# A decoder step on one core: the 128-fold copy of the relative-bias rows is made in DRAM from a 12 KB scratch

## The reference, cut to what matters

```python
def run_layer(x, c, mixer, w_ada, b_ada, ...):
    sh1, sc1, gt1, sh2, sc2, gt2, sh3, sc3, gt3 = adaln_params(c, w_ada, b_ada)   # silu(c) @ w_ada + b_ada
    x = x + MACARON * gt1 * swiglu(modulate(x, g_ffn1, sh1, sc1), w1_ffn1, w3_ffn1, w2_ffn1)
    heads, state = mixer(modulate(x, g_mix, sh2, sc2))
    x = x + gt2 * (heads @ w_out)
    x = x + MACARON * gt3 * swiglu(modulate(x, g_ffn2, sh3, sc3), w1_ffn2, w3_ffn2, w2_ffn2)
```

```python
    b = bias[jnp.clip(delta, 0, nk)]          # delta = query - key, bias = rel_bias[bucket of the distance]
    s = s + jnp.transpose(b, (2, 0, 1))
```

## Time and profile before

| | us |
|---|---|
| median of 3 runs | 2632.72 (2629.66 to 2635.13) |
| the profiled execution, its own time | 2627.94 |
| its span, first to last instruction | 2625.9 |
| around the span | 2.0 |
| TensorE busy | 2461.6 (94% of the span) |
| VectorE / ScalarE / GpSimd busy | 1163.8 / 905.3 / 44.5 |
| mean granted TensorE clock | 0.973 |
| mean busy share of the 16 DMA engines in the slice of the page that holds 224 us (of 40 slices) | 0.7 |

### The profile page before, as it was taken

The page is one execution under the profiler, slowest core; times in us unless marked ns, Lnnn a source line. Parts: engine busy times, 40 slices in busy tenths (PEclk is TensorE's granted clock), DMA queues, the critical chain, the costliest instruction groups (busy, mean ns, idle before and its releaser), DMA issues.

```text
span 2625.9 us, 56952 instructions
## 1 busy us (share of the span) xinstructions
PE 2461.6 (94%) x23011; PEld 2337.8 (89%) x23011; DVE 1163.8 (44%) x1802; ACT 905.3 (34%) x1099; POOL 44.5 (2%) x86
## 2 busy tenths in 40 slices
PE   5897999999999999899998767897999999999999
PEld 4797999999999999899996434697999999999999
DVE  2443444444444445666642112355444444444444
ACT  2332322323223234666531112335333333333332
POOL 0031000000000000000000000000000000000000
PEclk8999999999999999899999979898999999999999
DMA  8987777777787754344458999743444444454444
GB/s 326 397 318 240 273 294 295 278 286 282 296 301 279 285 194 167 113 160 149 178 204 325 385 370 408 300 173 113 167 168 163 163 171 160 160 176 160 163 161 160
DMA packets 111298, 614.50 MB, mean 234 GB/s; under 512 B 16224, under 2 KB 22640, under 8 KB 62304
## 3 DMA queue, kind: packets, MB, share of 16 engines
q1 hardware_dynamic: 107136, 603.81, 62.6%
q0 software_dynamic: 4064, 9.26, 1.3%
HBM read 604.36 MB, written 8.66 MB: 233 GB/s over the span
## 4 chain that ended last, share of the span: by engine, by line
PE 87%; DMA 7%; SPq 2%; DVE 2%; ACT 1%; issue 1%; ACTq 0%; DVEq 0%
PE banks L618 26%; PE banks L619 25%; PE banks L620 25%; PE banks L538 5%; DMA adax<-in_w_ada_dram 2%; SPq L473 1%; DMA kv_h<-in_vpool_dram 1%; PE banks L889 1%; DMA adaw<-in_w_ada_dram 1%; DMA kv_raw<-in_wink_dram 1%; DMA kv_z<-in_wink_dram 1%; PE banks L846 1%; SPq L464 1%; PE banks L708 1%; PE banks L832 0%
## 5 line engine op out<-in xcount | busy, mean ns | idle before, releaser
L618 PE MATMUL banks<-h_hi,w_hi 128*128 128x288 f32 x3696 | 1095.3, 296 | 26.4 <-DVE h_lo L1204 21.3
L619 PE MATMUL banks<-h_lo,w_hi 128*128 128x288 f32 x3696 | 1092.7, 296 | 0.0
L620 PE MATMUL banks<-h_hi,w_lo 128*128 128x288 f32 x3696 | 1091.6, 295 | 0.0
L1172 DVE TENSOR_TENSOR w_lo<-raw,w_hi 128x1024 fp32r<-128x1024 f32 (+2 forms) x670 | 764.1, 1181 | 500.9 <-ACT w_hi L927 493.7
L927 ACT ACTIVATE w_hi<-raw 128x1024 fp32r<-128x1024 f32 (+2 forms) x670 | 673.8, 1026 | 819.0 <-PE banks L620 599.7
L618 PEld LDWEIGHTS banks<-h_hi,w_hi 128*128 128x128 f32 x3696 | 697.4, 189 | 37.2 <-issue 33.2
L619 PEld LDWEIGHTS banks<-h_lo,w_hi 128*128 128x128 f32 x3696 | 697.3, 189 | 0.8
L620 PEld LDWEIGHTS banks<-h_hi,w_lo 128*128 128x128 f32 x3696 | 696.8, 189 | 0.0
L618 PE MATMUL banks<-g_hi,w_hi 128*128 128x288 f32 x1376 | 408.6, 297 | 0.0
L619 PE MATMUL banks<-g_lo,w_hi 128*128 128x288 f32 x1376 | 406.7, 296 | 0.0
L620 PE MATMUL banks<-g_hi,w_lo 128*128 128x288 f32 x1376 | 406.6, 295 | 0.0
(11 more groups left out here) (200 smaller groups left out, 1132.2 us busy)
## 6 DMA issues: line engine op xcount, KB each, us to landing
raw<-in_w_dram SPq DMA_DIRECT2D x166, 1024.0 KB, 4.9
adaw<-in_w_ada_dram SPq DMA_DIRECT2D x112, 1024.0 KB, 6.8
raw<-in_w_dram SPq DMA_DIRECT2D x64, 896.0 KB, 4.6
raw<-in_w_in_dram SPq DMA_DIRECT2D x49, 1024.0 KB, 4.9
adax<-in_w_ada_dram SPq DMA_DIRECT2D x32, 1024.0 KB, 12.8
raw<-in_w_dram SPq DMA_DIRECT2D x32, 960.0 KB, 4.7
raw<-in_w_out_dram SPq DMA_DIRECT2D x16, 1024.0 KB, 4.9
kv_raw<-in_kpool_dram SPq DMA_DIRECT2D x24, 512.0 KB, 7.2
```

Source lines behind the costliest of these rows:

```text
L618: pe.matmul(bank[:, 0:T], hi, m_hi[:, k, :], start=k == 0, stop=False)
L619: pe.matmul(bank[:, 0:T], hi, m_lo[:, k, :], start=False, stop=False)
L620: last = pe.matmul(bank[:, 0:T], lo, m_hi[:, k, :], start=False, stop=k == nk - 1)
L1172: dve.tensor_tensor(w_lo[:, r, a:b], raw[:, r, a:b], w_hi[:, r, a:b].bitcast(F32), ALU.subtract).then_inc(S["lo_ready"], 1)
```

## The change

POOL's one store of 1532 KB becomes two DMAs with a wait between them. The first writes the 8 rows once, into a new DRAM scratch `rev_rows` of 12 KB. POOL waits for it to land. The second makes the 128 copies of each row with `rev_rows` as its source and `rev_dram` as its destination, both in DRAM. POOL then waits for a count of 32 in place of 16. ScalarE's wait for a count of 16 stays as it was.

```diff
@@ -270,6 +270,7 @@
         rbs = sb("rbs", [32, HEADS])
         mx, nm, sm, rs = sb("mx", [P, 2]), sb("nm", [P, 2]), sb("sm", [P, 2]), sb("rs", [P, 2])
         pmx, psm = sb("pmx", [P, 2, 2]), sb("psm", [P, 2, 2])
+        rev_rows = nc.dram_tensor("rev_rows", [HEADS, REV], F32).ap()
         rev_dram = nc.dram_tensor("rev_dram", [HEADS, P, REV], F32).ap()
@@ -501,8 +502,10 @@
             pool.wait_ge(S["rev_ready"], 1)
-            pool.dma_start(rev_dram, rev[:, :].unsqueeze(1).to_broadcast([HEADS, P, REV])).then_inc(S["rev_stored"], 16)
+            pool.dma_start(rev_rows, rev[:, :]).then_inc(S["rev_stored"], 16)
             pool.wait_ge(S["rev_stored"], 16)
+            pool.dma_start(rev_dram, rev_rows.unsqueeze(1).to_broadcast([HEADS, P, REV])).then_inc(S["rev_stored"], 16)
+            pool.wait_ge(S["rev_stored"], 32)
             pool.wait_ge(S["h_ready"], H_END)
             pool.dma_start(selw[:, :], selh).then_inc(S["ld_selw"], 16)
```

## The result

| | before | after |
|---|---|---|
| median of 5 runs, us | 2634.87 | 2619.46 |
| ratio, with its 95% interval | | 0.9941 [0.9928, 0.9953] |
| the profiled execution, us | 2627.94 | 2615.63 |
| mean granted TensorE clock | 0.973 | 0.975 |

The change is 15.4 us faster (0.6%; by the interval, between 12.4 and 19.0 us); the forecast was 16.0 us. One of the five runs after took 2765.15 us, at a granted clock of 0.836, and the ratio leaves it out.

The account below looks back on a forecast made before the run. TensorE's stream of matmuls bounds the kernel (87% of the chain), so transfers matter only where it waits. Removing the 16.54 us dent and adding 0.5 us gives 2632.72 - 16.0 = 2616.7 us; 8 in 10 range 2612 to 2631.

Parts of the forecast that it names:

- The dent: First FFN loop, round at 248 us: one adaw wait and the slow matmuls behind it, 16.54 us, removed with the store.
- The store's price: Store from 8 neighbouring partitions: 713 ns a packet of 4.5 KB, one engine per row, eight engines at 6.3 GB/s each.
- slow end: Upper bound for the DRAM copy: no better than the store now, 196 KB at 6.3 GB/s, 31 us of each engine.
- rival B: No change: destination was the limit or the 12 KB source is as slow; same adaw wait, 2632.7 us; chance 0.14.
- The added store and its wait: 12 KB store and landing on POOL's queue: delays the large copy some 2 to 6 us, price on the path 0.
- The copy's price: DRAM to DRAM copy on eight engines at the pace of the toe load, 22 GB/s: 8.8 us of each.
- Rival A: Half the gain: the 12 KB source is slow to read, 17 us of each engine, 2623 us; chance 0.16.
- Rival C: Slower: copy packets hold engines over 713 ns, further rounds wait for adaw, about 2660 us; chance 0.10.
- What it costs TensorE: Wait for adaw left by the copy in the FFN loop: between 0 and 2.8 us, taken as 0.5 us.
- The sum: Whole kernel: 2627.94 - 16.54 + 0.5 = 2611.9 us for the profiled execution; 2632.72 - 16.0 = 2616.7 us against the median.

Follow-up runs that it names:

- Experiment 3: Kernel before, with the store from 8 partitions held back until TensorE has used the last w_ada pair, about 930 us: 2630.93 us, ratio 0.9988.
- experiment 1: The change, with the large copy read from the 8 SBUF partitions again, 12 KB store and wait kept: 2638.14 us against 2634.63, ratio 1.0016.
- Experiment 2: Kernel before, one store from SBUF, no scratch, but the 8 source rows on partitions 0, 4, ... 28: 2619.87 us, ratio 0.9947.
- experiments 5 and 6: Kernel before, one store from SBUF, source rows on partitions 0, 2, ... 14 (2618.38 us, ratio 0.9936) and 0, 16, ... 112 (2619.57 us, ratio 0.9939).
- experiment 8: The change with the copy on sixteen engines, its source 1532 KB of cached values in DRAM, each byte read once: 2616.17 us in one run.
- experiment 4: The change, with the copy written copy by copy (outer size 128, sixteen engines) in place of head by head: 2617.85 us, ratio 0.9941.
- experiment 7: The change, with the copy from DRAM held back until TensorE has used the last w_ada pair, about 930 us: 2618.71 us, ratio 0.9934.

## Why the prediction was right

**The dent.** The prediction read 16.54 us off the chain, 14.78 of waiting and 1.76 of slow matmuls, and put both down to the store. Experiment 3 shows that both come and go with it: the store moved, and a wait and a low clock appeared where it went. After the change both are gone but for 1.2 us.

**The store's price.** The 713 ns a packet and the eight engines were read from one row; experiment 1 has them again. The row is one window of 4 us, and the prediction let it stand for the whole store, 31 us of each of eight engines; in 226 to 270 us it is 198 us, about 25 each. This bears on the slow end and the rivals alone, not on the forecast. The prediction left open whether the source or the destination made it slow and gave the destination to rival B. Experiment 2 settles it for the source, and experiments 5 and 6 bear out the pattern of partitions behind it, for the stretches in which the store is slow. Rival B is out.

**The added store and its wait.** Priced at nothing on the path, and a start 2 to 6 us later. POOL waited 5.34 us, and the next thing it does is at 1055 us. Alone, in experiment 1, the later start made the wait longer by 2.6 us, within rival B's "2 to 4 us either way by the new phase", and the change gains in spite of it. It may not be free there either: experiment 2, whose store starts at 223.77 us with packets about as fast (181 against 191 ns), has no wait at all, and the change has 1.2 us. No run has the copy from DRAM at the earlier time.

**The copy's price.** Taken from the load of `toe`, 8.8 us of each of eight engines, "packets of some 200 ns", a landing in under 20 us. It is 191 ns and 19.9 us; 344 packets' worth of work (1532 KB in packets of 4.5 KB) on eight engines is 43 x 191 ns = 8.2 us each; the whole of 226 to 270 us gives 78 / 8 = 9.8, with the small loads. Rival A, with 17 us of each engine from a source that is slow to read, is out by this, and by experiment 8 the repeated read costs some 5% with sixteen engines. Rival C needed packets of more than 713 ns. Its ground, that every byte is both read from and written to DRAM, is not refuted: it may be what experiment 4 met with 336 ns.

**What it costs TensorE.** I chose 0.5 us between 0 and 2.8; it is 1.2. This is the one term of the sum with a size that was off, by 0.7 us. The second of the `adaw` loads of 235.93 landed after 13.3 us and not 5.9, so 7.4 us late against about 6 to spare. The prediction guessed that nothing would be left of the wait if a third of the copy fell before or after these loads. Some 0.7 of its 1.57 MB did fall before them, as POOL's queue in 226 to 236 us shows, and yet the wait came:

```profile
q0 software_dynamic: 570, 0.73, 25.9%
```

What the guess left out is the `raw` load that stands ahead of the two `adaw` loads in SP's queue. Here is the one issued in 231 to 233 us, with the change and with experiment 7, where no copy runs there:

```profile
raw<-in_w_dram SPq DMA_DIRECT2D x1, 1024.0 KB, 9.4
raw<-in_w_dram SPq DMA_DIRECT2D x1, 1024.0 KB, 4.9
```

Beside the copy it landed 4.5 us later, so the early part of the copy may have reached the `adaw` loads by way of the queue. How much of the 7.4 us came that way was not measured.

**The sum.** 16.54 - 1.2 = 15.3 us by the trace, 15.4 us by the medians. With an interval of about 3 us either way, so close an agreement with the forecast of 16.0 is in part luck. The forecast time, 2616.7 us, is 2.8 us under the 2619.46 measured; 2.2 of these are the median of the kernel before, 2632.72 of three runs and 2634.87 of five.

## What to carry to other kernels

A transfer that no engine waits for at that time can still set the kernel's time, if its packets are slow and run on the DMA engines that the next weights need; look for it where a load that usually takes 6 us takes 27. The price of a transfer on the other queues is the time that its packets hold an engine, not its bytes: count packets and share of the engines, in a window of a few us for the pace and over the whole transfer for the price. Look also at the loads that stand ahead in the same queue, for what is late there may be passed on. Where a few rows are stored from SBUF many times over, the choice of their partitions was worth a factor of four in a packet's time while the store was slow (713 against 181 ns), and of nearly three over the whole store (198 against 70 us). A small scratch in DRAM, or rows two, four or sixteen partitions apart, cured it equally well by the time of this kernel (2618.4 to 2619.9 us).

## What the runs showed that was not expected

Eight rows on partitions 0, 2, ... 14 and on 0, 16, ... 112 are about equally slow to store (342 and 309 ns a packet in 4 us), while 0, 4, ... 28 take 181 ns. But the slow level is not there from the start: with the step of 2 and eight engines at it, packets first took 198 ns. A copy from DRAM to DRAM lands earlier with more engines (13.1 against 19.9 us), but its packets are slower: on eight they take 191 ns beside the weights, on sixteen 336 ns with the engines to themselves, and the repeated read of one small source is not the reason. And the later start of the slow store alone, 5 us of phase against the loop, moved the time by 0.16% [0.07%, 0.26%] to the slow side.
